# Layers: one rotation per tile behind tiles ten to twelve, angles and sines a tile later; first mixer's head partners by VectorE's shuffle

## The reference, cut to what matters

```python
def apply_rope(x, cos, sin):                      # first mixer: 6 q heads, 2 k heads of 128
    xr = x.reshape(x.shape[:-1] + (2, 2, ROPE_FREQS))
    rot = jnp.concatenate([-xr[..., 1:, :], xr[..., :1, :]], axis=-2)
    return (xr * cos + rot * sin).reshape(x.shape)
q = apply_rope(rmsnorm(to_heads(q, N_Q_HEADS), q_norm_g[li]), cos, sin)
k = apply_rope(rmsnorm(to_heads(k, N_KV_HEADS), k_norm_g[li]), cos, sin)

def partial_rotary(x, positions):                 # second block: first 16 of 64 features
    ang = positions[..., None] * inv_freq
    cos, sin = jnp.cos(ang), jnp.sin(ang)
    rot = jnp.concatenate([x1 * cos - x2 * sin, x2 * cos + x1 * sin], axis=-1)

def compress(t, j):                               # second block: compressed keys and values
    z = (t[:, blk] + cmp_pos[j]).reshape(B, n_cmp, CMP_BLOCK * HD)
    return jax.nn.silu(z @ cmp_w1[j]) @ cmp_w2[j]
```

## Time and profile before

| | |
|---|---|
| median of 3 runs | 1968.36 us (1967.59 to 1972.19) |
| profiled execution: time, span | 1969.9 us, 1968.1 us |
| TensorE matmul busy | 1874.7 us, 95% of the span |
| TensorE weight load busy | 1475.2 us, 75% |
| VectorE busy | 1172.9 us, 60% |
| ScalarE busy | 824.3 us, 42% |
| GpSimd busy | 79.2 us, 4% |
| chain that ended last | PE 82%, DVE 11%, ACT 3%, issue 2%, DMA 1% |

### The profile page before, as it was taken

One profiled execution on the slowest core, in us unless ns is written; L12 is line 12 of the kernel. 1 busy time (PEld: TensorE's weight loads), 2 busy tenths in 40 slices (PEclk: granted clock), 3 DMA queues, 4 the chain that ended last, 5 costly groups with the idle time before them and its releaser, 6 DMA issues.

```text
span 1968.1 us, 25689 instructions
## 1 busy us (share of the span) xinstructions
PE 1874.7 (95%) x9722; PEld 1475.2 (75%) x9722; DVE 1172.9 (60%) x1971; ACT 824.3 (42%) x1373; POOL 79.2 (4%) x78
## 2 busy tenths in 40 slices
PE   6999998999999988999999999998999999999997
PEld 3867566887666766777988888876677798888886
DVE  5877668886889875556743234344564683323334
ACT  4554543343342343456643234224445663323422
POOL 0002100000202121000000000000000000000000
PEclk9999999999999999998999999998999999999999
DMA  9556035885001632111212222222211211323222
GB/s 368 198 187 255 0 122 212 315 314 196 16 5 34 243 141 88 63 65 65 71 59 107 92 100 89 103 107 86 86 44 65 87 65 65 107 85 107 85 107 86
DMA packets 45244, 230.77 MB, mean 117 GB/s; under 512 B 4985, under 2 KB 7034, under 8 KB 26972
## 3 DMA queue, kind: packets, MB, share of 16 engines
q1 hardware_dynamic: 45148, 229.48, 32.2%
HBM read 227.23 MB, written 2.10 MB: 117 GB/s over the span
## 4 chain that ended last, share of the span: by engine, by line
PE 82%; DVE 11%; ACT 3%; issue 2%; DMA 1%; SPq 0%; DVEq 0%; ACTq 0%
PE banks L2266 16%; PE banks L2267 16%; PE banks L2268 16%; PE banks L2529 3%; PE banks L2634 3%; PE banks L2636 3%; PE banks L2635 3%; PE banks L2549 2%; PE banks L2453 2%; PE banks L2664 1%; DMA w_raw<-in_wt 1%; PE banks L2676 1%; PE banks L2466 1%; PE banks L2690 1%; PE banks L2299 1%
## 5 line engine op out<-in xcount | busy, mean ns | idle before, releaser
L2266 PE MATMUL banks<-h_high,w_high 128*128 128x512 f32 x888 | 350.6, 395 | 7.2 <-DVE w_low L1393 3.5
L1393 DVE TENSOR_TENSOR w_low<-w_raw,w_high 128x1024 fp32r<-128x1024 f32 x180 | 220.1, 1223 | 230.4 <-ACT w_high L566 230.2
L2268 PE MATMUL banks<-h_high,w_low 128*128 128x512 f32 x888 | 346.3, 390 | 0.0
L2267 PE MATMUL banks<-h_low,w_high 128*128 128x512 f32 x888 | 346.3, 390 | 0.0
L566 ACT ACTIVATE w_high<-w_raw 128x1024 fp32r<-128x1024 f32 x180 | 189.8, 1054 | 148.6 <-PE banks L2268 123.3
L2266 PEld LDWEIGHTS banks<-h_high,w_high 128*128 128x128 f32 x888 | 167.1, 188 | 46.6 <-DVE w_low L1393 4.9
L2267 PEld LDWEIGHTS banks<-h_low,w_high 128*128 128x128 f32 x888 | 167.0, 188 | 36.1 <-issue 1.9
L2268 PEld LDWEIGHTS banks<-h_high,w_low 128*128 128x128 f32 x888 | 167.1, 188 | 35.1
L2266 PE MATMUL banks<-hidden_high,w_high 128*128 128x512 f32 x480 | 186.8, 389 | 0.0
L2267 PE MATMUL banks<-hidden_low,w_high 128*128 128x512 f32 x480 | 186.7, 389 | 0.0
L2268 PE MATMUL banks<-hidden_high,w_low 128*128 128x512 f32 x480 | 186.7, 389 | 0.0
(11 more groups left out here) (548 smaller groups left out, 3476.6 us busy)
## 6 DMA issues: line engine op xcount, KB each, us to landing
w_raw<-in_wt SPq DMA_DIRECT2D x129, 1024.0 KB, 5.0
mod_raw<-in_wmod SPq DMA_DIRECT2D x128, 512.0 KB, 5.0
mod_first<-in_wmod SPq DMA_DIRECT2D x8, 1024.0 KB, 11.6
cmp_w<-in_cmp_w SPq DMA_DIRECT2D x2, 2048.0 KB, 8.5
x<-in_xT SPq DMA_DIRECT2D x2, 1024.0 KB, 7.2
dft<-in_dft SPq DMA_DIRECT2D x2, 1024.0 KB, 7.6
out_x<-x SPq DMA_DIRECT2D x8, 256.0 KB, 2.1
hy_w<-in_hy_w SPq DMA_DIRECT2D x8, 192.0 KB, 3.2
```

The lines of the kernel that those rows point to most:

```text
L1393: v.tensor_tensor(low[:, :, :].rearrange("p k c -> p (k c)"), RAW[b // 2][:, b % 2, :], high[:, :, :].rearrange("p k c -> p (k c)").bitcas ...
L2266: mm(out, high[:, k, :], H[:, kk, :], start=start and k == order[0], stop=False)
L2267: mm(out, high[:, k, :], L[:, kk, :], start=False, stop=False)
L2268: last = mm(out, low[:, k, :], H[:, kk, :], start=False, stop=stop and k == order[-1])
```

## The change

In the first mixer TensorE's `rot` is gone, and `ROPE0` with it. VectorE makes the partner rows itself: `head_cos` gets a `stream_shuffle` of `zn` into `rope_b`, and `head_sin` multiplies `rope_b` in place of TensorE's bank. So that partners lie within 32 partitions, the host permutes the rows of the heads (weight columns, gains, cosine and sine tables); the sine table carries the sign.

In the second block's layers SyncE issues the pairs `(Q,1)` and `(Q+1,0)` ahead of `cmp_w1`, which comes in two halves, with the pairs `(Q+1,1)` and `(Q+2,0)` between them. The angles on VectorE stand one `tile_low` later, except for the first three steps (positions), which stand one earlier. ScalarE takes sine and cosine behind `tile_out(5)` in place of ahead of `tile_out(4)`, and makes `w_high` of tile 8 ahead of the `PAR` copies. `rope(0)` and `rope(1)` move behind `w_low` of tiles 9 and 10, `rope(2)` behind that of tile 12.

```diff
@@ SyncE, per layer
-            sp.wait_ge(w_used, lay * PER_LAYER + T_LAYERS - 1 + PRIME)
-            sp.dma_start(CW1[:, :], A["cmp_w1"][ds(lay * P, P), :]).then_inc(*did("in_cw1.all", 16))
-
-            with led.loop(sp, "layer_pairs", PER_LAYER // 4) as i:
+            first = lay * (PER_LAYER // 4) + T_LAYERS // 4
+            for c in range(2):
                 for half in (1, 0):
-                    load_pair(lay * (PER_LAYER // 4) + i + (T_LAYERS // 4 + 1 - half), half)
+                    load_pair(first + c + 1 - half, half)
+                if c == 0:
+                    sp.wait_ge(w_used, lay * PER_LAYER + T_LAYERS - 1 + PRIME)
+                sp.dma_start(CW1[:, 16 * P * c:16 * P * c + 16 * P], A["cmp_w1"][ds(lay * P, P), 16 * P * c:16 * P * c + 16 * P]).then_inc(*did(f"in_cw1.{c}", 16))
...
@@ ScalarE, layers
                     final_squares((2 * t - 4, 2 * t - 3))
-                    if t == 4:
-                        for c in range(2):
-                            act.wait_ge(*when(f"rot_arg.{c}"))
-                            nc.scalar.activation([SIN2, COS2][c], z(22 + c), ACT.Sin).then_inc(*did(f"rot.{c}"))
                 tile_out(t)
 
+            act.wait_ge(w_high, T + BLOB_AT + PRIME)
+            act.sem_inc(w_high, 2)
+            tile_high(8)
             act.wait_ge(w_loaded[1], 16 * (Q + 1) + 16)
             act.wait_ge(w_low, T + BLOB_AT + PRIME)
             for c in range(2):
                 nc.scalar.activation(PAR[:, c * D:(c + 1) * D], RAW[1][:, c, :], ACT.Copy).then_inc(w_low, 1)
-            act.wait_ge(w_high, T + BLOB_AT + PRIME)
-            act.sem_inc(w_high, 2)
-            tile_high(8)
             if lay == 0:
                 final_squares((6, 7))
             tile_out(5)
+            if lay == 0:
+                for c in range(2):
+                    act.wait_ge(*when(f"rot_arg.{c}"))
+                    nc.scalar.activation([SIN2, COS2][c], z(22 + c), ACT.Sin).then_inc(*did(f"rot.{c}"))
             act.sem_inc(w_used, 2)
...
@@ GpSimd, layers
-                pool.wait_ge(*when("rot.1"))
+                pool.wait_ge(*when("rot_arg.1"))
...
+            pool.wait_ge(*when("rp_k.3"))
...
@@ VectorE, first mixer
                 v.tensor_tensor(RA[j % 2][:, :], ZN[j % 2][:, :], COS0, mul).then_inc(*did(f"hn_ra.{j}"))
+                v.stream_shuffle(RB[j % 2][:, :], ZN[j % 2][:, :], PARTNER).then_inc(*did(f"hn_rot.{j}"))
...
-            v.tensor_tensor(RB[j % 2][:, :], bank(6 + j % 2), SIN0, mul).then_inc(*did(f"hn_rb.{j}"))
+            v.tensor_tensor(RB[j % 2][:, :], RB[j % 2][:, :], SIN0, mul).then_inc(*did(f"hn_rb.{j}"))
...
@@ VectorE, layers
-            tile_low(3)
             if lay == 0:
...
+            tile_low(3)
+            if lay == 0:
                 reduce_angle("rot_arg.0", "rot_red0", z(29), z(30), z(22))
             tile_low(4)
+            tile_low(5)
             if lay == 0:
                 reduce_angle("rot_arg.1", "rot_red1", z(29), z(30), z(23), float(np.float32(np.pi / 2)))
-            tile_low(5)
+            dve.wait_ge(w_low, T + 8 + PRIME)
             tile_low(8)
...
-            if lay == 0:
-                dve.wait_ge(*when("rot.1"))
...
-            rope(0)
-            rope(1)
             for t in LATER:
...
-                if t == 8:
-                    rope(2)
+                if t == 8 and lay == 0:
+                    dve.wait_ge(*when("rot.1"))
+                if t in (8, 9):
+                    rope(t - 8)
...
                         v.scalar_tensor_tensor(MO[:, m, :], bank((3, 6)[m]), -1.0 / 64, z(19 + m), mul, add).then_inc(*did(f"gm_c.{m}"))
+                    rope(2)
...
@@ TensorE, first mixer and layers
-                mm(bank(6 + j % 2), ROPE0, ZN[j % 2][:, :], start=True, stop=True).then_inc(*did(f"hn_rot.{j}"))
...
-                pe.wait_ge(*when("in_cw1.all"))
+                pe.wait_ge(*when(f"in_cw1.{c}"))
```

More of the change, by code:

```diff
@@ L2428, in _ @@
                 head_sum(j)
-            for j in heads_at(t - 1):
-                rot(j)
         def values_to_tokens(js):
@@ L2958, in tables @@
     place = np.stack([(t // 64).astype(f), (t % 64).astype(f)])
-    d = np.arange(P)
+    d = paired_rows()
     ang = (place[d // 64] * inv[d % 32][:, None]).astype(f)
-    rope = np.zeros((P, P), f)
-    for i in range(P):
-        rope[i + 32 if i % 64 < 32 else i - 32, i] = -1.0 if i % 64 < 32 else 1.0
     cnt = np.zeros((P, 2, S), f)
```

27 lines of the change are left out of this document (14 added, 13 removed).

## The result

| | before | changed |
|---|---|---|
| median | 1968.99 us (1967.59 to 1972.19, 4 runs) | 1949.72 us (1945.01 to 1950.40, 4 runs) |
| profiled execution: time, span | 1969.9, 1968.1 | 1949.99, 1947.9 |

The ratio is 0.9893 with an interval of 0.9875 to 0.9910: the changed kernel is 19.3 us faster. The forecast was 11.8 us and 1956.5, with a range down to 1952.0. The direction was right, the size was not, and the time lies 2.3 us outside the range.

A forecast was written before the change was run, and what follows sets the result against it. TensorE, busy 95% of the span, was taken as the bound. First mixer 0.7, layer one 7.2 and layer two 3.9 sum to 11.8 us, giving 1956.5 us, with a range of 1952 to 1961.5.

The forecast's parts named there:

- The step that failed: Layer one, tile 8: the raise stands behind ScalarE's whole list, sines included; start at 744.1 for 745.61, gain 1.5 us.
- its 7.2: Layer one's summed gain over tiles 2 to 9: 7.2 us, bounds 4.5 and 9.
- The first mixer: Shuffles replace rotations; TensorE idles some 4 us ahead of tile 14 and its clock falls; 0.7 us gained.
- The wait ahead of tile 10: First mixer: TensorE would wait for VectorE's `w_low` ahead of tile 10, a sign of being right; no size given.
- rival C: First mixer: the clock falls once more at the 1.4 us gap ahead of tile 11; 1.4 us more, 1958; chance 0.05.
- Rival B's first case: First mixer: clock stays up ahead of tile 14, gain 2.15 for 0.7 us, 1955; chance 0.17 with its second case.
- The forecast's rule that a gap of 2 us or more costs 1.3 to 1.45 us besides: TensorE: idleness of 2 us or more lowers the clock, costing some 1.3 to 1.45 us more than the gap.
- Tile 9: Both layers: no wait ahead; layer one starts 5.8 us earlier, tile 1.4 shorter; layer two 3.12 and 1.24.
- Rival D: Both layers: raise ahead of tile 8 comes late; at 1.6 us late the time is 1961; chance 0.13.
- E's landing: Both layers, tile 8: load lands late; 10.3 us eats the gain, 16.1 gives 1980, slower; chance 0.04.
- Rival F: Layers, tile 9: VectorE still late with `w_low`; layer one gives 2, sum 6.6 us, 1961.8; chance 0.05.
- GpSimd's collision: Layer one: GpSimd's sum of squares may block VectorE's `w_low` of tile 5, adding about 1 us ahead of tile 8.

The follow-up runs named there:

- raise_waits: Changed kernel, with ScalarE in layer one waiting for the second sine before the raise for tile 8: 1956.10 us, ratio 0.9931 to the kernel before.
- sines_last: Changed kernel, with the table load and two sines behind the raise in ScalarE's list: 1950.57 us, ratio 0.9906 to the kernel before.
- loads_back: Changed kernel, with SyncE's old order, all of `cmp_w1` ahead of the layer's pairs: 1952.98 us, ratio 0.9914 to the kernel before.
- ropes_back: Changed kernel, with the layers' rotations at their old places, two ahead of `w_low` of tile 9: 1963.88 us, ratio 0.9972 to the kernel before.
- mixer_alone: Kernel before, with only the first mixer's part of the change (shuffles on VectorE, no rotations on TensorE): 1966.11 us, ratio 0.9988.
- layers_alone: Kernel before, with only the second block's part of the change: 1952.38 us, ratio 0.9914.
- units_idle: Changed kernel, with two of tile 12's modulation units in VectorE's idle time ahead of `zn`, one behind `w_low` of tile 14: 1948.17 us, ratio 0.9894.

## Why the prediction was right in direction and too small

**The step that failed** is, in the part on layer one, "Behind it ScalarE's list is `w_high` 1.06, the two parameter copies 2.01, two squares 1.14, `tile_out` 0.57, a table load 1.28 and two sines, as large as two squares, 1.14: 743.4, and with 0.2 taken for the raise 743.6." The list is right up to `tile_out`. But the raise is no work of ScalarE's, it only adds to a semaphore, and it went while the table load and the sines were still to be done. The list is taken in its written order all the same; what the raise does not wait for is the end of the work ahead of it. Without the 2.4 us of these the same sum gives 741.2; I took 744.1, so 2.9 too late. The forecast stage was shorter by 1.5, the measured one by 4.2. And since the gap was 0.82, not 4 to 5, the clock did not fall, which gave 1.5 more behind tile 8. These two, 2.7 and 1.5, are the 4.3 by which layer one exceeded its 7.2, but for 0.1. `raise_waits` shows it by adding the wait that I had assumed, `sines_last` by removing the order that I had feared.

The Trainium skill states the rule that I overlooked: PSUM — Partial Sum Buffer, section "Engine vs sequencer instructions", says that an instruction of the sequencer alone waits only until earlier ones are dispatched, not until they complete. The trace agrees: 0.19 us after `tile_out`, with 2.4 us of work still to be done.

That step alone would have moved the forecast to 1952.2, at the edge of the range. The time lies outside it because of the 3.4 us in stretches without an edit. They have two places. Between 310 and 350 us TensorE's clock falls in every kernel, but not at the same matmuls: in the window from 340 to 350 the granted clock was 0.83 before, 1.00 in the changed kernel, and 0.83 again in `loads_back`, whose code is the changed kernel's up to 700 us. Between the waits at about 270 and 480 us the same code took 209.2 to 209.9 us in six executions and 211.3 and 211.7 in `ropes_back` and `loads_back`; before it took 211.4. So some 2 us of it come and go with the execution. The other place is ahead of layer one, where ScalarE waits for a load of weights. ScalarE's timeline, before:

```profile
694.50 1.06 ACT L566 ACTIVATE w_high<-w_raw 128x1024 fp32r<-128x1024 f32 x1 [5.00 <-DMA w_raw<-in_wt]
```

and in the changed kernel:

```profile
689.13 1.06 ACT L571 ACTIVATE w_high<-w_raw 128x1024 fp32r<-128x1024 f32 x1 [2.31 <-DMA w_raw<-in_wt]
```

In `mixer_alone` it waits 2.37, in `layers_alone` 4.34. So about 1 us here goes with the first mixer's part, 500 us behind it. By what way was not settled. What is left, 1.0 ahead of layer two less 0.5 at the end, was not traced; in `mixer_alone`, which has the code of before there, the stretch ahead of layer two is shorter by 2.5.

**Right.** The first mixer gave 0.84 where 0.7 was forecast, and in the way described: gaps ahead of tiles 11 and 14 in place of rotations, and the lower clock. That the sizes met is luck. Tile 14 started 1.1 earlier than worked out (147.39 for 148.5): 0.37 of it lay ahead of tile 4, where nothing was edited, 0.3 is the shuffle, which took 0.64 in place of 0.70, five times before tile 11, and the rest was not traced. The fall of the clock cost 2.4 instead of 1.45 in this execution and 2.5 in `raise_waits`; in the seven others with this gap (3.75 to 3.83 us) it cost 1.6, and their stage gives 1.25 to 1.35. The wait ahead of tile 10, also named as a sign, did not occur. The wait ahead of tile 11, 1.36 us, left the clock alone, so rival C was wrong. Rival B's first case, that the clock would stay up behind the gap at tile 14, occurred in none of the nine. `units_idle` took away the gap and the fall together, so it does not say what the clock alone is worth.

The forecast's rule that a gap of 2 us or more costs 1.3 to 1.45 us besides, by its length alone, does not hold. In `mixer_alone` TensorE waited 2.07 us ahead of tile 8 of layer one and 3.10 ahead of tile 9 of layer two, where it had waited 2.00 and 3.12 before, and the clock stayed up behind both. The latter row, and the window behind it:

```profile
1383.78 0.50 PE L2626 MATMUL banks<-h_high,w_high 128*128 128x512 f32 x1 [3.10 <-DVE w_low L1860]
...
1383.70:1387.70 4.00, 3.92 (x17) 3.23 (x18) 3.87 (x8) 0.00 (x0) 0.00 (x0) 1.00 0.69 238
```

and the window behind the 3.12 us before:

```profile
1391.20:1395.20 4.00, 3.97 (x11) 3.23 (x12) 3.87 (x7) 0.00 (x0) 0.00 (x0) 0.63 0.70 242
```

So 1.3 to 1.45 us is what a fall cost at these places when it came. That it came behind every such gap of the changed kernel's first mixer is measured, not a rule.

Tile 9 went as forecast: 4.2 by the gap and 1.5 by the clock in layer one (forecast 4.3 and 1.4), 3.3 and 1.4 in layer two (3.1 and 1.2), and tile 8 of layer two lost 0.36 (0.45). The loads' new order was put at 1.61 and was worth 2.1 at the tile, 1.5 over the stage. Rival D and E's landing did not occur in the changed kernel, where the load came in time; in `ropes_back` it landed at 7.3 us, and tile 8 waited 3.00 us for it. Rival F did not occur: ahead of tile 9 there is no wait, and the rotations fit behind the `w_low` buffers.

GpSimd's collision occurred one tile earlier than feared. VectorE's timeline of the changed kernel, `w_low` of tiles 4 and 5:

```profile
723.25 2.31 DVE L1866 TENSOR_TENSOR w_low<-w_raw,w_high 128x1024 fp32r<-128x1024 f32 x1
...
726.59 1.23 DVE L1866 TENSOR_TENSOR w_low<-w_raw,w_high 128x1024 fp32r<-128x1024 f32 x1 [1.03 <-ACT w_high L920]
```

GpSimd summed squares from 721.72 to 724.49, and the `w_low` of tile 4 took 2.31 us; its next sum began at 727.15, behind the start of the `w_low` of tile 5, and that took 1.23. The forecast's 0.5 between the two cases was not needed. But it had let both waits for the angles go, and 0.64 us ahead of tile 4 (725.62) stayed.

## What to carry to other kernels

Split an engine's list into work and signals before you add up a chain through it: a raise that only adds to a semaphore is priced by the last completion that its reader really waits for, not by all that stands ahead of it. Then look at the length of the gap that is left, for a gap that becomes short can give back its low clock too, and one that grew from 0.82 to 3.40 us made the tile behind it 1.3 us longer. Do not take a fall of the clock in one profile for a fixed price: compare several executions of the same code. And work that is moved to fill an engine's idle time also moves when buffers come free: the loads' order has to move with it (1948.17 without, 1945.06 with it).
